# Loading x1 as 120 and 8 partitions and storing half of the results as 30 and 2 in a decoder layer with product-key retrieval

## What is computed

```
mod = silu(c) @ w_ada + b_ada               -> shift1, scale1, gate1, shift2, scale2, gate2
x1  = x + gate1 * (mixer(modulate(rms_norm(x, g1), shift1, scale1) @ w_in) @ w_out)
h2  = modulate(rms_norm(x1, g2), shift2, scale2)
per token: 8 heads, each the 16 best of 128 x 128 experts by product keys
ffn = sum over the 128 chosen experts of  gate * gelu(h2 . expert_down[e]) * expert_up[e]
out = rms_norm(x1 + gate2 * ffn, g_final)
```

## Time and profile before

| What | us |
|---|---|
| median of 3 runs | 2830.8 |
| the profiled execution | 2833.91 |
| its span, first to last instruction | 2832.1 |
| TensorE busy, of the span | 1938.6 |
| VectorE busy | 1894.8 |
| ScalarE busy | 1210.7 |
| GpSimd busy | 1123.1 |

### The profile page before, as it was taken

How to read it: one execution, slowest core, us unless ns; L and a number is a source line. 1 busy time by engine, 2 the same in 40 slices (tenths; PEclk the granted TensorE clock), 3 DMA queues, 4 the chain that set the end, 5 groups by cost and what they waited for, 6 DMA issues and landing times.

```text
span 2832.1 us, 38640 instructions
## 1 busy us (share of the span) xinstructions
PE 1938.6 (68%) x13316; PEld 893.8 (32%) x13316; DVE 1894.8 (67%) x4714; ACT 1210.7 (43%) x3867; POOL 1123.1 (40%) x1030
## 2 busy tenths in 40 slices
PE   5898898888886566666656666665666666665553
PEld 4555354444442222232323222221322323221110
DVE  5686776785766567677666757677676756676454
ACT  1245445454453344454444434444343544344333
POOL 0044334344443254444444444444444444344342
PEclk9998898899886566665666667665766666576555
DMA  9899999999999999999999999999999999999997
GB/s 404 339 373 403 396 413 417 409 420 420 420 401 397 416 422 421 421 421 421 421 421 421 421 421 419 416 421 421 417 415 421 419 421 416 421 415 421 421 420 294
DMA packets 169221, 1162.38 MB, mean 410 GB/s; under 512 B 19009, under 2 KB 25665, under 8 KB 35778
## 3 DMA queue, kind: packets, MB, share of 16 engines
q0 software_dynamic: 147456, 1073.81, 91.9%
q1 hardware_dynamic: 21570, 86.11, 7.7%
HBM read 1151.97 MB, written 7.86 MB: 410 GB/s over the span
## 4 chain that ended last, share of the span: by engine, by line
DMA 54%; PE 22%; DVE 11%; ACT 6%; issue 3%; SPq 3%; POOL 0%; another core or an unknown queue 0%; DVEq 0%; POOLq 0%; ACTq 0%
DMA work<-experts,expert_rows 41%; DMA more_ring<-experts,expert_rows 8%; PE ps_sum L900 7%; DVE work L1560 5%; PE ps_small L866 5%; PE ps_m L815 4%; DMA work<-w_ada 2%; PE ps_m L759 2%; DMA weights<-experts,expert_rows 1%; ACT diag L1137 1%; ACT weight L1132 1%; DMA vn_u<-x_scratch 1%; PE ps_wide L841 1%; SPq L613 1%; PE ps_m L770 1%
## 5 line engine op out<-in xcount | busy, mean ns | idle before, releaser
L650 POOL DMA_INDIRECT work<-experts,expert_rows x818 | 899.0, 1099 | 1378.7 <-PE ps_sum L900 1225.8
L1560 DVE CUSTOM_DVE_ANT_0 work<-work 128x1024 f32<-128x1024 f32 x818 | 997.5, 1221 | 589.3 <-DMA work<-experts,expert_rows 573.4
L900 PE MATMUL ps_sum<-work,diag 128*32 128x256 f32 x6544 | 717.5, 523 | 674.7 <-ACT diag L1137 653.6
L1130 ACT ACTIVATE act_out<-act_in 128x1 f32<-128x1 f32 x1024 | 207.4, 203 | 1162.8 <-DVE act_in L1560 1141.9
L900 PEld LDWEIGHTS ps_sum<-work,diag 128*32 128x32 f32 x6544 | 150.1, 126 | 1146.5 <-ACT diag L1137 1052.1
L1137 ACT ACTIVATE diag<-const,weight 128x32 f32<-128x32 f32 x1024 | 329.2, 321 | 33.5
L1132 ACT ACTIVATE weight<-gate,act_out 128x1 f32<-128x1 f32 x1024 | 301.6, 295 | 33.3
L866 PE MATMUL ps_small<-h_t,weights 128*128 128x128 f32 x1344 | 291.2, 384 | 0.0
L866 PEld LDWEIGHTS ps_small<-h_t,weights 128*128 128x128 f32 x1344 | 249.3, 278 | 125.7 <-issue 120.4
L1560 DVE CUSTOM_DVE_ANT_0 more_ring<-more_ring,work 128x1024 f32<-128x1024 f32 x122 | 149.1, 1222 | 91.5 <-DMA more_ring<-experts,expert_rows 90.4
L650 POOL DMA_INDIRECT more_ring<-experts,expert_rows x122 | 134.8, 1105 | 180.3 <-PE ps_sum L900 175.5
(11 more groups left out here) (200 smaller groups left out, 1991.1 us busy)
## 6 DMA issues: line engine op xcount, KB each, us to landing
work<-w_ada SPq DMA_DIRECT2D x12, 2048.0 KB, 23.6
work<-sides SPq DMA_DIRECT2D x26, 576.0 KB, 8.4
work<-experts,expert_rows POOLq DMA_INDIRECT x818
weights<-sides SPq DMA_DIRECT2D x16, 576.0 KB
more_sides<-sides SPq DMA_DIRECT2D x12, 576.0 KB
weights<-w_in SPq DMA_DIRECT2D x3, 2048.0 KB, 17.2
x_buf<-x SPq DMA_DIRECT2D x8, 512.0 KB, 11.4
weights<-w_out SPq DMA_DIRECT2D x2, 2048.0 KB, 37.5
```

Source lines behind the costliest of these rows:

```text
L650: nc.gpsimd.indirect_dma_start(ring[x.ring], None, experts, bass.IndirectOffsetOnAxis(ap=rows_flat[:, x.column:x.column + 1], axis=0),).th ...
L900: last = nc.tensor.matmul(ps_sum[quarter(c), x.group, :], diag[:, x.ring, :], ring[x.ring][:, D + c * QCOLS:D + (c + 1) * QCOLS], start=x. ...
L1130: nc.scalar.activation(act_out[:, s:s + 1], act_in[:, s:s + 1], ACT.Gelu).then_inc(s_gelu, 1)
L1560: nc.vector.tensor_tensor_reduce(down, down, h2_spread[x.segment % 2], 1.0, 0.0, ALU.mult, ALU.add, act_in[:, x.g % TURN:x.g % TURN + 1]). ...
```

## The change

The loads of x1 for tiles 3 to 6 are each issued as two DMAs, partitions 0 to 119 and 120 to 127. Of the four stores of tiles 0 to 6, the first two (quarters 0 and 1) are each issued as two DMAs, of 30 and of 2 partitions; quarters 2 and 3 and all of tile 7 stay as they are. The bytes moved and their order in the loop are the same; there are 4 loads and 14 stores more. Counts on the semaphores follow: 32 for a load, 96 for a stored tile.

```
+FEW_ROWS, FEW_QROWS = 120, 30
+WHOLE_STORES = (2, 3)
+STORED = 16 * (2 * QUADS - len(WHOLE_STORES))
...
-                    sp.dma_start(x1_kept[t][:, :], x1_dram[t]).then_inc(s_x1k[t % 2], 16)
+                    for rows in (slice(0, FEW_ROWS), slice(FEW_ROWS, P)):
+                        sp.dma_start(x1_kept[t][rows, :], x1_dram[t][rows, :]).then_inc(s_x1k[t % 2], 16)
                     return
                 if t >= 2:
-                    sp.wait_ge(s_out, 64 * (t - 1))
+                    sp.wait_ge(s_out, STORED * (t - 1))
...
                 for c in range(QUADS):
-                    sp.dma_start(out_v[t, c][:, first:end, :], y[quarter(c), first:end, :]).then_inc(s_out, 16)
+                    cut = QROWS if c in WHOLE_STORES or t == TILES - 1 else FEW_QROWS
+                    for lo, hi in ((0, cut), (cut, QROWS)):
+                        if lo < hi:
+                            sp.dma_start(out_v[t, c][lo:hi, first:end, :],
+                                         y[c * QROWS + lo:c * QROWS + hi, first:end, :]).then_inc(s_out, 16)
...
-            sp.wait_ge(s_out, 64 * (TILES + 1))
+            sp.wait_ge(s_out, STORED * (TILES - 1) + 2 * 16 * QUADS)
...
-                    pe.wait_ge(s_x1k[t % 2], 16 * ((t - KEPT_FROM) // 2 + 1))
+                    pe.wait_ge(s_x1k[t % 2], 32 * ((t - KEPT_FROM) // 2 + 1))
```

More of the change, by code:

```diff
@@ L1378, in stats2 @@
                 elif t >= KEPT_FROM:
-                    dve.wait_ge(s_x1k[t % 2], 16 * ((t - KEPT_FROM) // 2 + 1))
+                    dve.wait_ge(s_x1k[t % 2], 32 * ((t - KEPT_FROM) // 2 + 1))
                 elif t:
@@ L1436, in norm2 @@
                 if t >= KEPT_FROM:
-                    dve.wait_ge(s_out, 64 * (t - 1))
+                    dve.wait_ge(s_out, STORED * (t - 1))
                 nc.vector.reciprocal(stat[:, 5:6], stat[:, 4:5]).then_inc(s_norm2, 1)
@@ L1574, in scale_sums @@
                 else:
-                    dve.wait_ge(s_out, 64 * t)
+                    dve.wait_ge(s_out, STORED * t)
                 nc.vector.tensor_tensor(y[:, first:end, :], ps_sum[:, first:end, :],
```

## The result

The changed kernel takes 2843.6 us (median of 6 runs, 2839.73 to 2845.65) against 2830.93 before (6 runs); the ratio is 1.0041, 95% interval 1.0030 to 1.0051. It is slower by 0.4%, 12.7 us between the medians, where 4.4 us faster were forecast and the range ended at 2832.5. The profiled execution took 2839.73 us with a span of 2837.9; it is the shortest of the six.

What follows compares the result with a forecast made beforehand. The DMA engines bound the kernel, with one last engine 5.0 us behind the next. Relieving it by 8.9 us counts 5.0, less 0.6 for the second engine: 2830.8 - 4.4 = 2826.4 us, range 2823.5 to 2832.5.

Steps and rivals of the forecast that it cites:

- What bounds the kernel: Whole span: DMA engines busy 99.6%, about 421 GB/s; in the tail one engine 5.0 us behind the next sets the end.
- Who carries the rows: Split loads and stores: 120 and 30 partitions go to 15 engines, 8 to eight, 2 to two; one engine is relieved.
- the rival of a cut dealt otherwise: Split DMAs: 120 partitions over 12 engines, 30 over 10, 3.4 us more for each; about 2829 us; chance 0.05.
- the price of a KB: Load moved between engines: priced at 25 to 26.3 GB/s an engine, so 224 KB take 9.2 or 8.7 us.
- The 8.9 us of relief: Left-out engine: 224 KB less in loads and stores; if it is last, only 5.0 us count, less 0.6: gain 4.4.
- the weakest step: Tail: the choice that the engine left out, at the end of the dealing order, is the one that ends last.
- The rival for this: Tail: the engine left out is not the last; no gain, 2831.4 us or 2833.6 us; chance 0.17.
- The issues: SyncE's queue: 18 DMAs more, 8 us spread over 2200 us, cost nothing; tile 3 has no cover.
- the rival of the stall: Tile 3: issues add 11.7 us before x1 is in, 6.2 us lost; 2837.0 us, or 2832.6 with the gain; chance 0.06.
- The rival's 5.5 us to spare: Tile 3: gathers queued last till about 972, the next is issued at 966.45, so 5.5 us of stall cost nothing.
- The sign for a relieved last engine: Tail windows: one engine alone, at share 0.06, for less than 2 us in place of 5.
- windows of the body stay at 421: Body windows: share stays at 1.01 and rate at 421 GB/s, named as a sign of the forecast.

Runs made afterwards that it cites:

- e6: Kernel before with all four stores of tiles 0 to 6 split 30 and 2, loads whole; slot 384 to 1023 takes 1617.8 us.
- e2: Changed kernel with whole loads of x1, only the two stores a tile split 30 and 2; first median 2833.5 us.
- e11: Second run of the changed kernel with whole loads, two stores a tile split 30 and 2; 2830.57 us, ratio 0.9998 to the kernel before.
- e8: Kernel before with all stores of tiles 0 to 6 as two pieces of 16 partitions; slot 384 to 1023 takes 1618.0 us.
- e1: Changed kernel with whole stores, only the loads of x1 split 120 and 8; ratio 1.0038 to the kernel before.
- e9: Kernel before with two stores a tile (tiles 0 to 6) as pieces of 7, 7, 7, 7, 4 partitions; slot 384 to 1023 takes 1622.8 us.
- e7: Kernel before with all stores of tiles 0 to 6 as four pieces of 8 partitions; slot 384 to 1023 grows by 6.6 us.
- e5: Kernel before with each load of x1 as two column halves of 128 partitions, stores whole; 416 to 420 GB/s, no median given.

## Why the prediction was wrong

**What bounds the kernel** was read rightly: the bytes per second of the 16 engines, and in the tail one engine 5 us behind the next. Both stand in the profile after.

**Who carries the rows.** The numbers of engines were right: 15, 8 and 2, by the count of packets above, which rules out the rival of a cut dealt otherwise (12 and 10 engines). But that 120 partitions go over fewer engines was taken as a shift of load and no more. This is the step that failed, twice.

First, the price of a KB. The sum took 25 to 26.3 GB/s an engine for the load of x1 and nothing for its neighbours, as if it did not matter which engine writes which partition. It measured 2.5 us a load, 7.5 us in the stretch, and has its share in what was lost at tile 3, where x1's packets take 207 ns for 159 and the gathers' 394 for 314. No term of the sum and no rival held it, though the nearest rows were in the trace before: loads of 32 partitions at 359 to 374 GB/s. I had looked at the 128-partition load and at the time of issues, not at the bandwidth behind a DMA that spans fewer than 128.

Second, whom it relieves. The 8.9 us of relief went to an engine that is not the last: one engine is still alone for 5.1 us, and e6, which takes 6.2 us off the engine left out, ends its stretch at 1617.8 as before. The gain of 4.4 us was nothing; the choice of the last place in the order, called the weakest step, was wrong. The rival for this, 2831.4 us for an engine among the first eight, names the mechanism that came: e2, e6 and e11 stay at the time before. Had only the stores been split, the measured 2830.57 would have lain in the range, by luck, with the wrong engine relieved.

**The issues.** More of them showed no cost in the body (e8 has 28 more). At tile 3, where nothing covers the load, the rival of the stall came in part. SyncE's rows, beside the earlier trace rows:

```profile
557.20 2.21 SPq L564 DMA_DIRECT2D out<-h_next  x6
...
903.08 19.15 SPq L564 DMA_DIRECT2D out<-h_next  x6
922.33 8.66 SPq L538 DMA_DIRECT2D vn_u<-x_scratch  x2
1232.47 2.19 SPq L564 DMA_DIRECT2D out<-h_next  x6
1234.76 0.72 SPq L538 DMA_DIRECT2D x_buf<-x_scratch  x2
```

Four stores took 16.64 us, six take 19.15, the load 8.66 for 3.32, and VectorE's wait grows by 4.1 us: 14.2 against 10.1, with 11.4 when only the load is split (e1) and 10.6 and 11.5 when only the stores are (e2, e11). The prediction had it within 1 us of 10.1. The rival's 11.7 us of queue were 7.9. Its price of 4.2 us for a store was too high, as two more took 2.5, and its 3.3 us for a load too low, as one more took 5.3. Nor is it bytes alone that hold the queue: with the same bytes eight stores of 16 partitions hold it for 18.6 us (e8) and eight of 30 and 2 for 26.4 (e6); what sets it stays open.

The rival's 5.5 us to spare were not there. Against the kernel before, VectorE's wait is longer by 4.1 us in the changed kernel, 8.0 in e9 and 12.5 in e7, and slots 256 to 320, with 190.6 us before, take 5.6, 7.4 and 12.2 us more (196.2, 198.0, 202.8): nearly every microsecond of the wait is lost by the kernel. e2, e5, e8 and e11 take 192.1 to 192.7 there, so that the changed kernel's loss at tile 3 is 4 to 6 us. With 7.5 that makes 11 to 13 us, which is the 12.7 between the medians.

**What would show it.** The sign for a relieved last engine, less than 2 us alone at 0.06, stayed out, as the prediction said it would if the wrong engine was relieved. The sign "windows of the body stay at 421" was the one that caught the cause.

## What to carry to other kernels

When gathers over 128 partitions keep all DMA engines busy and a load into SBUF has to be cut, try the cut by columns first: here it left the rate as it was, while every load that spanned fewer than 128 partitions slowed itself and the gathers beside it. Stores that span fewer showed nothing of this here. Before load is moved between engines, find out which engine is late, by a dose that shifts it the other way; and look at GB/s behind each DMA, because here the busy share stayed at 1 while a quarter of the rate was gone. And count the slack of a wait in more than one way: the 5.5 us that rows seemed to give were not there.

## What the runs showed of the hardware that I had not expected

- A load of 512 KB over 120 and 8, 64 and 64 or 112 and 16 partitions took the core from 422 GB/s to between 284 and 322 in the worst 4 us, and the fall lasts as long as the load's packets do, some 8 us; the same bytes as two column halves left it at 416 to 420.
- The direction matters: stores of 32, 30, 8, 7 and 4 partitions from SBUF did not lower the rate (418 to 422 GB/s in windows of 16 and 20 us over them), loads of 32 did (359 to 374).
- A DMA leaves one packet of 4 bytes for each engine that it uses, as far as all thirteen other kernels' counts show (14, 28, 42, 48, 64, 112, 224 and 448 more all fit): the packets on the page tell over how many engines a cut was dealt.
- One engine ends 5 us behind the next in nearly every kernel with evenly dealt stores (gap 5.0 to 5.4 us, only in e5 3.9), and the doses place it, by the assumed dealing, at the third or fourth place. What makes it slow stays open.
